# One block-fused kernel: the scan's first triangular inverse moved into the SSD stage, y times z at the evacuation, two barriers removed, the wout weights fetched later

## The chip, the cores and the metric

The kernel runs on one core of a Trainium2 chip. The metric is device time in microseconds (us). The core has TensorE (PE) for matmuls, VectorE (DVE), ScalarE (ACT), GpSimd (POOL) for elementwise work, and SyncE (SP), which only issues DMAs; ACT issues DMAs too. Each engine works its own instruction list in order and waits for others at semaphores.

## The reference

Two transformer-like blocks on 512 latent tokens. Only the first one's token mixers matter here. It projects the normalised input, runs a Mamba-2 style SSD scan and a gated DeltaNet (GDN) scan in two directions, gates and normalises both, and multiplies with `w_out`:

```
p = modulate(rmsnorm(x)) @ w_in          # z, xbc, dt, q k v, gate, a, beta
# SSD: chunks of 128 tokens, 16 heads
y = einsum(scores, xdt) + einsum(C, h_prev) * exp(acum);   ssd = xs * D + y (both directions)
v = ssd * silu(z);  v = v * rsqrt(mean(v * v over 512 channels)) * g
# GDN: T = I + strict(k_beta k^T * decay);  sol = triangular_solve(T, [v*b, k_beta*exp(g)])
v_new = u - w @ S;  o = q_dec @ S + qk @ v_new;  S = S * d + k_dec^T @ v_new
x = x + g1 * (concat(ssd_norm, gdn_norm(o) * silu(gate)) @ w_out)
```

Everything is float32. A large matmul takes its weights and its input as a high and a low part (`whi`, `wlo`), three passes for each product.

## The kernel before

**Stages.** The weights of all projections come as units of 128x1024 through two buffers: SP loads `raw`, ACT writes `whi` (L403 or L1786), DVE writes `wlo` (L410 or L2468), PE multiplies. The stages this text speaks of, with their place in the profiled execution, are these:

1. The zg stage, to 525 us: 16 units, first the 8 of z, then the 8 of the gate. PE runs one unit (24 matmuls) each round; ACT evacuates it (L1716) and stores it to `zg_scratch` (L1718). Beside it run the GDN pair masks (`AT`, stored to `at_scratch`), the SSD chunk states, and on DVE the inverses of the 32x32 diagonal blocks: `inverse_steps(n)` eliminates two columns (L2286, L2290) for the chains 0 and 1 (n below 16) or for chain 2 (n from 16). Their blocks (`UB`) come by small DMAs: most from SP (L741), 16 from ACT (`first_diagonals`, L1694).
2. `barrier(eng, 1)` (L355 to L358): PE, ACT, DVE and POOL drain, count up `phase_end` and wait until all four have. ACT first waits for its last stores to `zg_scratch`.
3. The SSD stage, 532 to 622 us: 4 chunks (`ci`) of 8 head pairs (`hp` on DVE and ACT, `b` on PE). For a pair PE makes the decays (L1100, L1101), ACT exponentiates them into `lbuf` (L1750, four), DVE makes `wmat` (L2383, L2384), PE makes y (L1117, L1120, L1125). PE makes the decays two pairs ahead. At a chunk's start stand the scores (L1085, ACT copies them to `stb`) and four selections (L1093) that DVE turns into `cpm` (L2373). ACT evacuates y into `yfm` (L1758), two halves for each chunk. `inverse_steps(16)` to `(31)` of chain 2 run on DVE from pair 2 of chunk 0 to pair 1 of chunk 2. SP then stores the inverses to `xb_scratch` and `xv_scratch` (L780 to L792).
4. `barrier(eng, 2)`.
5. The start of the GDN scan, 622 to 660 us. A scan step works on 4 groups `q`: 2 directions and 2 halves of the heads. A step's full inverse is put together from the 32x32 blocks by PE in four parts: `corner5` and `block5` (L1155), `corner6` and `block6_t` (L1179), with ACT copying corners to `PM` (L1774) and DVE copying blocks (L2409, L2412, L2419) between. Their operands are the mask `C` and the scattered blocks `DT`, `DB` (7 DMAs from SP for each q, L805 and L810, into buffers cleared before). For step 0 all this stands after the barrier and in front of the loop; so do z (loaded back whole, Silu, L1813), y times z (L2479), the squares (L1829), their sums (L1254), the roots (L1833 Ln, L1835 Exp), and the scaling with `ssdn` (L2484).
6. The scan, 660 to 789 us: steps 0 to 5, each `state_read` (L1220), `new_values` (L1138), `output` from step 2 on (L1239, L1240), `state_step` (L1138), `key_rows` (L1200), with the inverse parts of the next step between. At step 1 SP stores `yfm` to `y_scratch`; it comes back as `ynb` at the end.
7. The wout stage, from 789 us: units 0 to 5 take y (`yshi`, `yslo`), the others the GDN heads, which ACT and DVE normalise meanwhile (L1905, L1833, L1835, L1917, L2527, L2534). Units 0, 1 and 2 are loaded in the zg stage; unit 0 is split there and unit 1 after the second barrier.

**What sets the order.** All is written out by hand; there is no scheduler.

Of the kernel before, what the change touches and what calls it, by code (L numbers as in the profile page):

```python
# [18 lines left out]
P = 128  # L19
D = 1024  # L20
# [89 lines left out]
def layout(x, c, ctx, c_ctx, w_mod, b_mod, norm1_g, w_in, ssd_conv_w, ssd_conv_b, ssd_dt_bias, ssd_A_log,  # L110
# [22 lines left out]
    stream = {"qkvx": units(w_in, cols), "zg": units(w_in, np.concatenate([oz + r(1024), og + r(1024)]))}  # L133
# [101 lines left out]
def build_kernel(nc, a, out):  # L235
    ctx = ExitStack()
    with ctx:
# [106 lines left out]
        dve_done, act_done, phase_end = sem("dve_done"), sem("act_done"), sem("phase_end")  # L344
# [9 lines left out]

        def barrier(eng, n):  # L355

            eng.drain().then_inc(phase_end, 1)
            eng.wait_ge(phase_end, 4 * n)  # L358
# [72 lines left out]
        def room(n):  # L431
# [11 lines left out]
        grow = [at(f"grow{x}", kb, (P, 512), F32R) for x, kb in enumerate((203.125, 205.125, 164, 166, 168, 170, 76, 78))]  # L443
# [3 lines left out]
        S, DB0, DT1, DB1, C = ([at(f"{n}{q}", 36 + 8 * i + 2 * q, (P, 512)) for q in range(4)]  # L447
                              for i, n in enumerate(("S", "DB", "DT1", "DC", "C")))
        DB = (DB0, DB1)
        PM, DT0, KD, VN, QE, QKD, VB = ([at(f"{n}{q}", kb + 2 * q, (P, 512)) for q in range(4)] for n, kb in (  # L450
            ("PM", 140), ("DU", 148), ("KD", 156), ("VN", 164), ("QE", 172), ("QKD", 180), ("VB", 188)))
        DT = (DT0, DT1)
        ofm = at("ofm", 81, (P, GH * LAT))
# [18 lines left out]
        z_silu, gate_silu = ksum_full, tap_ready  # L472
        z_silu_0, gate_silu_0 = GH, 34
# [39 lines left out]

        def dcol(d, c, h=0):

            return (d * NCH + c) * NH + h
# [31 lines left out]
        zs = at("zs", 172, (P, KB * LAT))  # L548
        rsy = [at(f"rsy{g}", 203.125 + 2 * g, (P, LAT)) for g in range(2)]
        ynb = [at(f"ynb{s}", kb, (P, 4 * LAT)) for s, kb in enumerate((44, 156))]  # L550
# [116 lines left out]
        def _(sp_):  # L667
# [76 lines left out]
            for b in range(16):  # L744
# [5 lines left out]
                if b == 5:  # L750
                    sp_.wait_ge(v_stored, 16)
                if 5 <= b < 9:
                    load_diagonals(b - 5, 0)
                if b == 9:
                    load_diagonals(2, 1)
                    load_diagonals(3, 1)
# [15 lines left out]

            for job, j in tail[:3]:
                tail_load(job, j)
# [18 lines left out]

            store_inverse(0, (0,))
            store_inverse(1, (1,))
# [24 lines left out]
            def load_inverse(t, q):  # L820

                sp_.wait_ge(p5_full, 4 * (t - 1) + q + 1)
                if t == 1:
                    sp_.wait_ge(zeroed, 4 + q + 1)
                    sp_.wait_ge(db_zeroed, 4 + q + 1)
                else:
                    sp_.wait_ge(dr_full, 4 * (t - 2) + q + 1)
                    sp_.wait_ge(p6_full, 4 * (t - 2) + q + 1)
                load_dt(t, q)
                load_d32(t, q)  # L830

            sp_.wait_ge(zeroed, 4)
            sp_.wait_ge(xb_stored, 32)
            sp_.wait_ge(xv_stored, 32)
            for q in range(4):
                load_dt(0, q)
            store_mixed()
            sp_.wait_ge(phase_end, 8)
            sp_.wait_ge(db_zeroed, 4)
            for q in range(4):  # L840
                load_d32(0, q)
            for q in range(4):
                load_inverse(1, q)
# [13 lines left out]
            sp_.wait_ge(p6_full, 24)  # L857
            sp_.wait_ge(y_spilled, 16)
# [4 lines left out]
            sp_.dma_start(v3(gate, KB), zg_dram[KB:2 * KB].rearrange("b p n -> p b n")).then_inc(back_loaded, 16)  # L863
# [3 lines left out]
            for job, j in tail[3:]:  # L867
                tail_load(job, j)
# [11 lines left out]
        def _(pe):  # L880
# [198 lines left out]
            barrier(pe, 1)  # L1079

            for ci in range(4):
                c = NCTX + ci
                need(sc_copied, 1, lag=1)
                for gr in range(2):
                    mm = pe.matmul(bank[gr][:, 0:P], bf[64 * gr:64 * gr + 64, c * P:(c + 1) * P],  # L1085
                                   cfm[64 * gr:64 * gr + 64, ci * P:(ci + 1) * P], start=True, stop=True)
                mm.then_inc(sc_full, 1)
                if ci == 0:
                    pe.wait_ge(row_parts, 9)
                for m in range(4):  # L1090
                    need(cp_ready, 1, lag=2)
                    i = ci % 2 * 4 + m
                    pe.matmul(bank[2 + m % 2][:, :], halfsel[i // 4][:, i % 4 * P:(i % 4 + 1) * P], grow[4 + ci // 2][:, :], start=True, stop=True  # L1093
                              ).then_inc(cp_full, 1)

                def decays(hp):

                    need(l_ready, 1, lag=2)
                    bk = bank[4 + hp % 2]
                    pe.matmul(bk[:, :], cbf(0), b4(cbf(1, 2), 2), start=True, stop=False)  # L1100
                    pe.matmul(bk[:, :], rowcol(ci % 2 * 8 + hp), grow[2 + ci // 2][:, :], start=False, stop=True).then_inc(l_full, 1)  # L1101

                decays(0)
                decays(1)

                for b in range(KB):
                    if b + 2 < KB:
                        decays(b + 2)
# [1757 lines left out]
```

## Time and profile before

| | us |
|---|---|
| median of 3 runs | 2484.76 (2472.23 to 2487.89) |
| the profiled execution | 2470.89 |
| its span, first to last instruction | 2469.1 |
| PE busy | 2291.1 (93%) |
| DVE busy | 1354.3 (55%) |
| ACT busy | 984.4 (40%) |
| POOL busy | 150.7 (6%) |

In the rows further down a line of the timeline holds its start, its duration, the engine (SPq and ACTq are DMA issues), line of code, operation, output and input tiles, shape, count, and in brackets how long the engine stood idle before it and what released it. PEclk is the granted TensorE clock as a share of 2.4 GHz: 1.00 is 2.4 GHz and 0.50 is 1.2 GHz.

### The profile page before, as it was taken

The page shows a single profiled execution, that of the slowest core. Times are in us where ns is not written, and L with a number is a line of the kernel's source. Part 1 is how long each engine was busy: PE and PEld are TensorE (multiplying, and loading weights), DVE is VectorE, ACT ScalarE, POOL GpSimd, SP SyncE. Part 2 cuts the span into 40 slices and gives each one's busy share as a digit, 9 for nine tenths or more (in the row PEclk, how much of TensorE's full clock was granted, in tenths as well). Part 3 has the DMA queues.
Part 4 walks back from the last instruction along what each step waited for, and adds up shares of the span by engine and source line. Part 5 has one row for each costly group of instructions (what it writes and reads, how often), then busy time and mean ns, then how long its engine had stood idle before and what let it go on. Part 6 is the DMA issues. An engine that isn't in the chain of part 4 may idle for free.

```text
span 2469.1 us, 31028 instructions
## 1 busy us (share of the span) xinstructions
PE 2291.1 (93%) x12406; PEld 1831.3 (74%) x12406; DVE 1354.3 (55%) x2106; ACT 984.4 (40%) x1610; POOL 150.7 (6%) x108
## 2 busy tenths in 40 slices
PE   3899899989699889999998999999999899999997
PEld 2788787765588668888876568888888657888885
DVE  8566687677677345434455644444354564434445
ACT  3445455344524633322454544222234464322222
POOL 0000000000000010000032001000011302000002
PEclk9989999986899989999999999999999999999998
DMA  6233524630555223232232112232223202232232
GB/s 247 103 109 113 188 86 157 183 117 18 156 159 190 68 83 99 95 99 97 95 100 62 41 35 94 95 101 94 97 93 100 68 10 69 94 103 94 95 100 79
DMA packets 114495, 252.26 MB, mean 102 GB/s; under 512 B 45040, under 2 KB 45808, under 8 KB 113584
## 3 DMA queue, kind: packets, MB, share of 16 engines
q1 hardware_dynamic: 100896, 229.56, 28.1%
q10 hardware_dynamic: 13456, 20.71, 2.5%
q8 instruction: 99, 1.62, 0.3%
q14 instruction: 44, 0.36, 0.0%
HBM read 225.07 MB, written 25.17 MB: 101 GB/s over the span
## 4 chain that ended last, share of the span: by engine, by line
PE 78%; DVE 8%; ACT 6%; issue 3%; DMA 3%; SPq 1%; ACTq 1%; POOL 0%; DVEq 0%
PE bank L1306 18%; PE bank L1308 18%; PE bank L1307 18%; PE bank L966 4%; DVE cacc L2159 1%; DMA raw<-in_s_qkvx 1%; PE bank L1468 1%; PE bank L1457 1%; PE bank L1138 1%; PE bank L965 1%; DMA modw<-in_w_mod 1%; PE bank L1061 1%; PE bank L1063 1%; PE bank L1062 1%; PE bank L1125 1%
## 5 line engine op out<-in xcount | busy, mean ns | idle before, releaser
L1786 ACT ACTIVATE whi<-raw 128x1024 fp32r<-128x1024 f32 (+1 forms) x267 | 277.7, 1041 | 924.0 <-PE bank L1308 919.5
L1306 PE MATMUL bank<-ahi,whi 128*128 128x512 f32 x1152 | 454.6, 395 | 8.9 <-DVE alo L2588 6.0
L1307 PE MATMUL bank<-alo,whi 128*128 128x512 f32 x1152 | 450.6, 391 | 0.0
L1308 PE MATMUL bank<-ahi,wlo 128*128 128x512 f32 x1152 | 450.4, 391 | 0.0
L2468 DVE TENSOR_TENSOR wlo<-raw,whi 128x1024 fp32r<-128x1024 f32 (+1 forms) x267 | 327.3, 1226 | 132.8 <-ACT whi L1786 132.4
L1306 PE MATMUL bank<-bhi,whi 128*128 128x512 f32 x736 | 286.5, 389 | 0.0
L1308 PE MATMUL bank<-bhi,wlo 128*128 128x512 f32 x736 | 286.3, 389 | 0.0
L1307 PE MATMUL bank<-blo,whi 128*128 128x512 f32 x736 | 286.3, 389 | 0.0
L1306 PEld LDWEIGHTS bank<-ahi,whi 128*128 128x128 f32 x1152 | 217.7, 189 | 60.0 <-issue 11.3
L1307 PEld LDWEIGHTS bank<-alo,whi 128*128 128x128 f32 x1152 | 217.8, 189 | 46.1 <-issue 1.4
L1308 PEld LDWEIGHTS bank<-ahi,wlo 128*128 128x128 f32 x1152 | 217.7, 189 | 45.6
L2800 POOL TENSOR_TENSOR accx<-accx,sqr 128x512 f32<-128x512 f32 x42 | 72.3, 1722 | 1548.0 <-ACT sqr L1873 1342.7
L1306 PEld LDWEIGHTS bank<-bhi,whi 128*128 128x128 f32 x736 | 138.2, 188 | 28.9 <-issue 0.3
L1307 PEld LDWEIGHTS bank<-blo,whi 128*128 128x128 f32 x736 | 138.2, 188 | 28.7
L1308 PEld LDWEIGHTS bank<-bhi,wlo 128*128 128x128 f32 x736 | 138.2, 188 | 28.7
L2546 DVE TENSOR_TENSOR xr<-bank,xr 128x512 f32<-128x512 f32 x64 | 44.3, 692 | 159.5 <-PE bank L1308 159.5
L410 DVE TENSOR_TENSOR wlo<-raw,whi 128x1024 fp32r<-128x1024 f32 x51 | 62.3, 1222 | 95.5 <-ACT whi L403 95.2
L403 ACT ACTIVATE whi<-raw 128x1024 fp32r<-128x1024 f32 x51 | 54.1, 1063 | 150.6 <-DMA raw<-in_s_qkvx 76.6
L966 PE MATMUL bank<-hhi,whi 128*128 128x512 f32 x272 | 109.3, 402 | 0.0
L966 PE MATMUL bank<-hhi,wlo 128*128 128x512 f32 x272 | 108.4, 399 | 0.0
L966 PE MATMUL bank<-hlo,whi 128*128 128x512 f32 x272 | 108.1, 398 | 0.0
L2159 DVE SCALAR_TENSOR_TENSOR cacc<-cbuf,vec,cacc 128x784 f32<-128x784 f32 (+1 forms) x102 | 98.2, 963 | 10.7 <-ACT cacc L1611 7.9
(434 smaller groups left out, 3663.2 us busy)
## 6 DMA issues: line engine op xcount, KB each, us to landing
raw<-in_s_gu SPq DMA_DIRECT2D x88, 512.0 KB, 3.3
raw<-in_s_qkvx SPq DMA_DIRECT2D x34, 512.0 KB, 4.6
late_modw<-in_w_mod SPq DMA_DIRECT2D x32, 512.0 KB, 3.7
raw<-in_s_up SPq DMA_DIRECT2D x32, 512.0 KB, 3.3
raw<-in_s_down SPq DMA_DIRECT2D x32, 512.0 KB, 3.3
raw<-in_s_dn SPq DMA_DIRECT2D x32, 512.0 KB, 3.3
raw<-in_s_win SPq DMA_DIRECT2D x24, 512.0 KB, 3.3
raw<-in_s_zg SPq DMA_DIRECT2D x16, 512.0 KB, 3.5
```

Of the source, the lines that this page charges most:

```text
L403: act.activation(whi[k][:, 0:kc * P], raw[k][:, 0:kc * P], ACT.Identity).then_inc(hi_ready, 1)
L410: dve.tensor_tensor(wlo[k][:, 0:kc * P], raw[k][:, 0:kc * P], whi[k][:, 0:kc * P].bitcast(F32), ALU.subtract).then_inc(lo_ready, 1)
L965: pe.matmul(cx, w, x[:, s, 0:CTX], start=first, stop=last)
L966: mm = pe.matmul(lat, w, x[:, s, CTX:TOK], start=first, stop=last)
L1306: pe.matmul(out, w_hi, x_hi, start=start, stop=False)
L1307: pe.matmul(out, w_hi, x_lo, start=False, stop=False)
L1308: return pe.matmul(out, w_lo, x_hi, start=False, stop=stop)
L1786: act.activation(whi[u % 2][:, 0:width[u + 2] * P], raw[u % 2][:, 0:width[u + 2] * P], ACT.Identity).then_inc(hi_ready, 1)
L2159: after(dve.scalar_tensor_tensor(out=acc, in0=x, scalar=w, in1=acc, op0=ALU.mult, op1=ALU.add))
L2468: dve.tensor_tensor(wlo[u % 2][:, 0:width[u + 2] * P], raw[u % 2][:, 0:width[u + 2] * P], whi[u % 2][:, 0:width[u + 2] * P].bitcast(F32), ...
L2546: dve.tensor_tensor(blk(xr, b), bk[:, :], blk(xr, b), ALU.add).then_inc(taken, 1)
L2800: pool.tensor_tensor(acc[:, :], acc[:, :], sqr[n % 2][:, :], ALU.add).then_inc(sq_added, 1)
```

## The change

- The zg stage computes the gate's 8 units first and z's 8 last, and ACT evacuates z with Silu. It has no unit of wout behind it any more. ACT's 16 DMAs for `UB` go to SP; the inverse steps of chains 0 and 1 start one unit later and run two each round (0 and 1 at unit 8, 14 and 15 at unit 15).
- Both barriers are gone; single waits take their place.
- In the SSD stage DVE evacuates y times z in one instruction (`y_times_z`), with z loaded back by chunk (`load_z`); POOL squares it (`y_square`) and clears `DB` and `DT`.
- The four parts of step 0's inverse run on PE in chunk 2 (pairs 4 and 6) and chunk 3 (pairs 3 and 5), with their copies on ACT (pairs 5 and 4) and DVE (at the end of chunks 2 and 3). The blocks of steps 0 and 1, and the values of step 0, are fetched during the SSD stage.
- The scan starts with the square sums (four matmuls for each half), key rows for two of four groups and `corner5` of step 1. The roots' two Ln stand together, then the two Exp; POOL applies the roots (8 multiplies); the factor `ssdn` moves into the split of y after the scan.
- `C` and `DB` of the scan and `zc` lie at 0 to 24 KB, where `raw`, `whi` and `wlo` are, so the wout units 0 and 1 are loaded after the scan's last inverse and split after its last `new_values`; unit 2 is loaded behind the residual input `xr`.

```diff
-            eng.drain().then_inc(phase_end, 1)
-            eng.wait_ge(phase_end, 4 * n)
...
+        C, DB0, S, KD, PM, DT0, DT1, VN, QE, QKD, VB = ([at(f"{n}{q}", kb + 2 * q, (P, 512)) for q in range(4)] for n, kb in (
+            ("C", 0), ("DB", 8), ("S", 36), ("KD", 52), ("PM", 140), ("DU", 148), ("DT1", 156), ("VN", 164), ("QE", 172),
...
@@ SP
-            for job, j in tail[:3]:
-                tail_load(job, j)
...
+            load_z(0)
+            load_z(1)
...
+            sp_.wait_ge(y_taken, 2)
+            load_z(2)
+            sp_.wait_ge(y_taken, 4)
+            load_z(3)
             store_mixed()
...
             sp_.wait_ge(p6_full, 24)
+            for job, j in tail[:2]:
+                tail_load(job, j)
...
-            for job, j in tail[3:]:
+            for job, j in tail[2:]:
@@ PE
+                part = {(2, 4): corner5, (2, 6): block5, (3, 3): corner6, (3, 5): block6_t}.get((ci, b))
...
+                if ci == 3:
+                    pe.wait_ge(dt64_ready, 4)
...
+            def square_sums(gr):
+                pe.wait_ge(y_taken, 7 + gr)
+                pe.wait_ge(q_ready, 7 + gr)
...
+            square_sums(0)
+            key_rows(0, 0)
+            key_rows(0, 1)
+            corner5(1, 0)
+            corner5(1, 1)
+            square_sums(1)
@@ ACT
-                if b in (6, 7):
-                    first_diagonals(b - 6)
...
-            for k in range(2):
-                act.wait_ge(zg_stored[k], 8 * job.n)
-            barrier(act, 1)
...
+                if (ci, hp) == (2, 5):
+                    act.wait_ge(xb_stored, 64)
+                    act.wait_ge(xv_stored, 64)
+                    for q in range(4):
+                        corner(0, q, p5_full)
+                if (ci, hp) == (3, 4):
+                    for q in range(4):
+                        corner(0, q, p6_full)
+                        load_corners(1, q)
@@ DVE
-                if b >= 7:
-                    for n in range(max(0, 2 * b - 15), min(16, 2 * b - 13)):
+                if b >= 8:
+                    for n in range(2 * b - 16, 2 * b - 14):
                         inverse_steps(n)
...
+                dve.tensor_tensor(y_part(ci, gr), h4(bank[6 + gr][:, :]), h4(zc[ci % 2][:, 512 * gr:512 * gr + 512]), ALU.mult).then_inc(y_taken, 1)
...
+                    if hp == 5:
+                        y_times_z(ci, 0)
+                    if hp == 1 and ci:
+                        y_times_z(ci - 1, 1)
+                if ci >= 2:
+                    for q in range(4):
+                        (block5, block6_t)[ci - 2](0, q)
+            y_times_z(3, 1)
@@ POOL
+                pool.tensor_tensor(h4(xtm[:, o:o + 512]), y_part(ci, gr), y_part(ci, gr), ALU.mult).then_inc(q_ready, 1)
...
+                pool.tensor_tensor(blk(yfm, b), blk(yfm, b), rsy[b // 4][:, :], ALU.mult).then_inc(yn_ready, 1)
```

Three places show how the instructions move. The first is SP's queue where the zg stage goes over into the SSD stage. Before:

```order
L715 DMA raw_49<-in_s_zg 128x1024 [waits lo_ready,hi_ready]
L715 DMA raw_50<-in_s_zg 128x1024 [waits lo_ready,hi_ready]
L771 DMA raw_49<-in_s_wout 128x1024 [waits lo_ready]
L771 DMA raw_50<-in_s_wout 128x1024 [waits lo_ready]
L771 DMA raw_49<-in_s_wout 128x1024 [waits lo_ready]
L780 DMA xb_scratch<-XB_137 128x1024 [waits inv_done0]
L783 DMA xv_scratch<-XT_140 128x1024 [waits inv_done0]
```

Now:

```order
L713 DMA raw_50<-in_s_zg 128x1024 [waits lo_ready,hi_ready]
L833 DMA C_174<-at_scratch 128x512 [waits lo_ready,hi_ready]
L833 DMA C_175<-at_scratch 128x512
L833 DMA C_176<-at_scratch 128x512
L833 DMA C_177<-at_scratch 128x512
L779 DMA xb_scratch<-XB_137 128x1024 [waits inv_done0]
L782 DMA xv_scratch<-XT_140 128x1024 [waits inv_done0]
L779 DMA xb_scratch<-XB_138 128x1024 [waits inv_done1]
L782 DMA xv_scratch<-XT_141 128x1024 [waits inv_done1]
L827 DMA zc_222<-zg_scratch 128x8x128 [waits zg_stored1,zg_stored0,unit_done]
```

The three wout loads have left; the masks of step 0 and, behind the stores of the inverses, the first z of the SSD stage stand there.

The second place is ACT in chunk 2 of the SSD stage, pairs 5 to 7 (each pair is a row and a row of three more). Before:

```order
L1750 ACTIVATE lbuf_157<-bank,ng 128x128 [waits w_ready,l_full]
L1750 ACTIVATE lbuf_157<-bank,ng 128x128 x3
L1758 ACTIVATE yfm<-bank 128x4x128 [waits y_full]
L1750 ACTIVATE lbuf_156<-bank,ng 128x128 [waits w_ready,l_full]
L1750 ACTIVATE lbuf_156<-bank,ng 128x128 x3
```

Now:

```order
L1805 ACTIVATE lbuf_157<-bank,ng 128x128 [waits w_ready,l_full]
L1805 ACTIVATE lbuf_157<-bank,ng 128x128 x3
L1772 ACTIVATE PM_190<-bank 128x512 [waits p5_full,xv_stored,xb_stored]
L1772 ACTIVATE PM_191<-bank 128x512 [waits p5_full]
L1772 ACTIVATE PM_192<-bank 128x512 [waits p5_full]
L1772 ACTIVATE PM_193<-bank 128x512 [waits p5_full]
L1805 ACTIVATE lbuf_156<-bank,ng 128x128 [waits w_ready,l_full]
L1805 ACTIVATE lbuf_156<-bank,ng 128x128 x3
```

The copy of y is gone; four corner copies stand between the exponentials of pair 5 and pair 6, behind a wait for PE and for the stores of chain 2's inverses.

The third place is ACT at the end of the scan. Before:

```order
L1779 ACTIVATE VN_208<-bank 128x512 [waits dr_full]
L1779 ACTIVATE VN_209<-bank 128x512 [waits dr_full]
L1860 ACTIVATE yshi<-ynb_227 128x512 [waits yn_loaded0]
L1860 ACTIVATE yshi<-ynb_227 128x512 x3
L1860 ACTIVATE yshi<-ynb_228 128x512 [waits yn_loaded1]
```

Now:

```order
L1816 ACTIVATE VN_204<-bank 128x512 [waits dr_full]
L1816 ACTIVATE VN_205<-bank 128x512 [waits dr_full]
L1823 ACTIVATE whi_51<-raw_49 128x1024 [waits unit_done,raw_loaded0]
L1823 ACTIVATE whi_52<-raw_50 128x1024 [waits unit_done,raw_loaded1]
L1870 ACTIVATE yshi<-ynb_228,vec 128x512 [waits yn_loaded0]
```

Two splits of wout stand between the last new values and the high part of y.

## Rows read from the trace of the kernel before

**Rows 1.** Stretches: from:to, length, busy PE PEld DVE ACT POOL, clock, DMA, GB/s.
```profile
460.00:480.00 20.00, 16.46 (x68) 13.27 (x66) 6.74 (x19) 4.11 (x6) 0.00 (x0) 0.83 0.60 162
...
532.10:557.40 25.30, 22.30 (x154) 12.57 (x154) 20.92 (x52) 10.20 (x36) 1.91 (x4) 0.70 0.07 11
557.40:585.80 28.40, 27.69 (x156) 15.70 (x154) 21.55 (x54) 10.68 (x36) 0.00 (x0) 0.50 0.00 1
585.80:605.00 19.20, 18.49 (x156) 10.37 (x154) 12.40 (x29) 10.62 (x36) 0.00 (x0) 0.82 0.21 56
605.00:622.40 17.40, 15.97 (x154) 9.21 (x152) 9.97 (x21) 10.52 (x36) 0.00 (x0) 1.00 0.00 1
```
**Rows 2.** Timeline of ACT in the zg stage: the diagonal DMAs and the late split.
```profile
462.94 5.76 ACTq L1694 DMA_DIRECT2D UB<-at_scratch  x8
468.80 1.06 ACT L403 ACTIVATE whi<-raw 128x1024 fp32r<-128x1024 f32 x1 [6.33 <-issue]
```
**Rows 3.** Chain of waits at the first barrier: start, duration, what.
```profile
526.01 6.00 DMA zg_scratch<-stg
```
**Rows 4.** Timeline of DVE at the start of chunks 0 and 3 of the SSD stage.
```profile
538.01 0.43 DVE L2383 TENSOR_TENSOR wmat<-lbuf 128x256 f32<-128x256 f32 x1 [1.43 <-ACT lbuf L1750]
...
605.94 2.57 DVE L2373 TENSOR_TENSOR cpm<-bank,cfm 128x512 f32<-128x512 f32 x4 [1.70 <-PE bank L1093]
...
609.51 0.42 DVE L2383 TENSOR_TENSOR wmat<-lbuf 128x256 f32<-128x256 f32 x1 [1.00 <-issue]
```
**Rows 5.** Timeline of PE at 2.4 GHz: two SSD pairs, then the scan's start.
```profile
599.19 0.39 PE L1100 MATMUL bank<-cb 128*128 128x512 bf16 x1
...
600.92 0.39 PE L1100 MATMUL bank<-cb 128*128 128x512 bf16 x1
...
657.01 2.84 PE L1254 MATMUL bank<-zs,cf 128*128 128x512 f32 x6
659.69 1.95 PE L1138 MATMUL bank<-VB,DU 128*128 128x128 f32 x16
661.57 0.45 PE L1155 MATMUL bank<-PM,DT 32*32 32x32 f32 x32
...
670.69 0.68 PE L1179 MATMUL bank<-DC,C 64*64 64x64 f32 x16
...
674.57 2.05 PE L1220 MATMUL bank<-S,kf 128*128 128x128 f32 x16
```
**Rows 6.** Timeline of SP: the last store of chain 2's inverse.
```profile
596.48 1.10 SPq L792 DMA_DIRECT2D xv_scratch<-XT  x1
```
**Rows 7.** Its time from issue to landing, from the answer on its line.
```profile
DMA to landing us min/median/max: 3.9/3.9/3.9
```
**Rows 8.** Timeline of DVE and POOL: one operation alone, then beside one of POOL.
```profile
1232.87 0.75 DVE L2553 SCALAR_TENSOR_TENSOR alo<-xr,fm,ahi 128x512 fp32r<-128x512 f32 x1
...
1238.31 1.88 DVE L2553 SCALAR_TENSOR_TENSOR alo<-xr,fm,ahi 128x512 fp32r<-128x512 f32 x1
1238.34 1.29 POOL L2800 TENSOR_TENSOR accx<-accx,sqr 128x512 f32<-128x512 f32 x1 [2.14 <-ACT sqr L1873]
```
**Rows 9.** Timeline of the copies on ACT and DVE at the scan's start.
```profile
640.00 1.08 ACT L1774 ACTIVATE PM<-bank 128x512 f32<-128x512 f32 x2 [1.95 <-PE bank L1155]
640.33 0.28 DVE L2409 COPY DB<-bank 32x128 f32<-32x128 f32 x1 [8.95 <-PE bank L1155]
640.64 0.64 DVE L2412 STREAM_TRANSPOSE DU<-bank 32x128 f32<-32x128 f32 x2
...
648.47 4.90 DVE L2479 TENSOR_TENSOR yfm<-yfm,zs 128x512 f32<-128x512 f32 x8
```
**Rows 10.** Timeline of SP and ACT at the start of the wout stage.
```profile
790.56 51.18 SPq L771 DMA_DIRECT2D raw<-in_s_wout  x7
...
795.37 1.06 ACT L1786 ACTIVATE whi<-raw 128x1024 fp32r<-128x1024 f32 x1 [1.31 <-PE bank L1308]
```
**Rows 11.** Issue to landing of the first of those loads, issued at 790.56.
```profile
DMA to landing us min/median/max: 8.8/8.8/8.8
```

More of the change, by code:

```diff
@@ L1130, in _ @@
-            barrier(pe, 2)
-            A, B = bank[0:4], bank[4:8]
-            def four(dst, w, x):
-                for j in range(4):
-                    o = slice(j * P, (j + 1) * P)
-                    mm = pe.matmul(dst[:, o], w[:, o], x[:, o], start=True, stop=True)
-                return mm
-            def key(t, q, j):
-                h, c = 4 * (q // 2) + j, GSEQ[q % 2][t]
-                return kf[:, h * TOK + c * P:h * TOK + (c + 1) * P]
+            A, B = bank[0:4], bank[4:8]
@@ L1193, in block6_t, with first_inverse @@
                 quadrants(False, PM, DT[t % 2], e6t_full, p)
+            def first_inverse(ci, b):
+                if (ci, b) == (2, 4):
+                    pe.wait_ge(sc_copied, 3)
+                    pe.wait_ge(row_parts, 11)
+                part = {(2, 4): corner5, (2, 6): block5, (3, 3): corner6, (3, 5): block6_t}.get((ci, b))
+                if part is corner6:
+                    pe.wait_ge(sc_copied, 4)
+                if part is not None:
+                    for p in range(2):
+                        part(0, p)
@@ L1195, in key_rows, with four, key @@
+            def four(dst, w, x):
+                for j in range(4):
+                    o = slice(j * P, (j + 1) * P)
+                    mm = pe.matmul(dst[:, o], w[:, o], x[:, o], start=True, stop=True)
+                return mm
+            def key(t, q, j):
+                h, c = 4 * (q // 2) + j, GSEQ[q % 2][t]
+                return kf[:, h * TOK + c * P:h * TOK + (c + 1) * P]
             def key_rows(t, q):
@@ L1854, in _ @@
                         load_corners(t + 2, q)
+            split(JOB["wout"].u0 - 2)
+            split(JOB["wout"].u0 - 1)
             for b in range(KB):
@@ L2492, in _ @@
                     for q in range(4):
+                        if t == 0 and q == 2:
+                            key_rows(0, 2)
+                            key_rows(0, 3)
                         block5(t + 1, q)
+                else:
+                    split(JOB["wout"].u0 - 2)
+                    split(JOB["wout"].u0 - 1)
                 if lat:
```

415 lines of the change are left out of this document (203 added, 212 removed).

## The prediction, made before the changed kernel ran

> **What bounds the kernel now.** The page gives PE 93% of the span, so the change can only pay where PE waits or runs at half clock. I read the windows by stage first, then the chain of waits, then the timelines at the seams. The stretches of the SSD stage [rows 1] show the granted clock: 0.50 in chunk 1, 0.70 and 0.82 in chunks 0 and 2, 1.00 in chunk 3. Chunk 1 takes 28.4 us and chunk 3 17.4 us with the same pairs. Chunk 1's row holds two things: PE is busy 27.69 of 28.4, because its work takes twice as long at 1.2 GHz, and DVE has 21.55 us of work against 9.97 in chunk 3, because the inverse steps run beside it. The chain shows one clear stop, 6.00 us for a store to land in front of the first barrier [rows 3]. After chunk 3 ends at 622.4, PE does its first `new_values` at 659.69 and its first state read at 674.57 [rows 5]: 52.2 us in which it mostly waits for blocks from DRAM, for copies between the parts of one inverse, and for z, squares and roots.
>
> **Term A, the zg stage.** ACT issues 16 diagonal DMAs itself, the first 8 in 5.76 us, and the split of the next unit stands idle for 6.33 behind them [rows 2]. From 460 to 480 PE is busy 16.46 of 20 us at a mean clock of 0.83 [rows 1]: 3.54 us idle, and since 0.83 means 6.8 us at half clock, 3.3 of its busy time ran at half and cost another 1.6. So 5.1 us are lost. The DMAs now stand in SP's queue, ahead of the loads of the gate and z units, and DVE's inverse starts one unit later. SP issues 8 such DMAs in about 5 us where ACT took 5.76, which fits a round of 6 to 8 us, though closely. I take -5; bounds 0 (SP is late instead) and -6.
>
> **Term B, the first barrier.** Its 6.00 us store wait [rows 3] goes, as the first reader of z is five pairs into chunk 0. What is late next is the chain over DVE's `fq`, ACT, DVE, the first `xd` and `cpm`. In chunk 3 the first `wmat` follows the first `cpm` by 609.51 - 605.94 = 3.6 us at full clock [rows 4]. The last of PE's work before the barrier ends at 526.1; I give the eps chain and `xd` 2.4 us, so `cpm` starts at 528.5 and `wmat` at 532.1, where it was at 538.01 [rows 4]: -6. Bounds -4 and -7. ACT's change of table between Silu and Exp stands ahead of waits it has anyway, so I cost it at nothing; uncovered it would be one activation or two, within the bounds.
>
> **Term C, work put into the SSD stage.** One pair takes PE 600.92 - 599.19 = 1.73 us at full clock [rows 5].
> - Chunks 0 and 1, close to the limit on both engines: DVE gets three y times z of 4.90/8 = 0.61 to 0.7 us [rows 9] and POOL three squares. A collision of DVE with a POOL operation that reads two tiles cost DVE 1.88 - 0.75 = 1.1 us [rows 8]. 3 x (0.7 + 1.1) = 5.4; DVE's spare time at the chunk's start takes some: +3.3, bounds 0 and +5.4.
> - Chunk 2: PE gets `corner5` and `block5`, 4 x 0.45 = 1.8 [rows 5]. ACT copies four corners, 2 x 1.08 = 2.2 us [rows 9], ahead of pair 6's exponentials, where PE is only one pair ahead; less what PE does meanwhile that is +1.3. Before, the stores behind those copies were issued until 597.6 and landed 3.9 later [rows 6, 7], 601.5; now a z load of 0.5 MB and a y times z stand ahead of them, 2 us, while ACT wants them at about 601.7: +1.8. At the chunk's end DVE does four copies with two transposes each, 4 x 0.99 = 4.0 [rows 9], and PE waits for them; 1.70 of it was idle before [rows 4]: +2.3. Sum +7.2, bounds +4 and +12.
> - Chunk 3: `corner6` and `block6_t`, 4 x 0.65 = 2.6 from [rows 5], and +0.9 for four small copies and four DMAs in ACT's queue ahead of pair 5. +3.5, bounds +2.6 and +6. The last four DVE copies lie behind the first square sums.
>
> C is +14, bounds +7 and +23.
>
> **A rule on the ports.** The Trainium skill (SBUF — State Buffer, Who interferes with whom) says that a DVE instruction with two SBUF inputs and a GpSimd instruction that reads SBUF exclude each other, the later one waiting for the whole of the other; the trace agrees, with 1.88 us against 0.75 [rows 8]. By that rule `wmat` and the inverse steps can meet each of the squares while y times z, with one input in PSUM, cannot.
>
> **Term D, from the end of chunk 3 to the first state read, 52.2 us.** Now PE does four square-sum matmuls for half 0. Three took 2.84 [rows 5], so four take 3.8. Then key rows for two groups 1.0, `corner5` of step 1 0.9, the second square sums 3.8: `new_values` begins at +9.5. y times z (0.7) and POOL's square (1.3, [rows 8]) of the last half are done by +3, under the first sums. Then 1.95 and 0.45 [rows 5], key rows 1.0, a wait of 1.7 until DVE, which has two block copies first, has made the key rows of groups 2 and 3, `new_values` 2.0 and `block5` 0.45: +17. From there to the state read it is as before: two state steps, two `corner6`, key rows and two `block6_t`, 8.3 us. State read at +25.3 instead of +52.2: -26.9. Bounds -20 (if the blocks of step 1 or POOL are late) and -29. POOL's eight root multiplies end later than DVE's did, up to 13.6 us at 1.7, and SP holds step 3's blocks behind the store of y; the gap to step 3's `corner5` covers that by some 2 us.
>
> **Term E, the start of the wout stage.** ACT has two splits more (1.06 each, [rows 10]), DVE too, but its y parts keep ahead of PE's unit 0. Then ACT must split unit 2, which before was long there. SP now issues its load behind `xr`. Before, the load in that place was issued at 790.56 and landed 8.8 later, at 799.4 [rows 10, 11]; ACT's split began at 795.37. ACT's chain of Ln and Exp for the eight heads follows it in order and PE waits for the heads, so +4; bounds +2 and +5.
>
> **Sum.** -5 - 6 + 14 - 26.9 + 4 = -19.9 us. The profiled execution took 2470.9; this makes 2451. It lies 13.9 under the median of the runs shown, 2484.8, and I put the same difference there: 2465.
>
> **Rivals.**
> - *The clock stays at 2.4 GHz through the SSD stage.* For it: PE no longer stands 6 us before chunk 0. Against it: the clock fell in the middle of chunk 0, after having been full, when DVE prepared chain 2, and that is unchanged. DVE's 21.55 us in chunk 1 plus its waits at the chunk's start bound it at some 25; chunks 0 and 2 would win about 5 together: -8 more, 2457.
> - The Trainium skill (TensorE: Matmul & The Clock Gate, What's actually happening) says that sustained activity releases the clock and idleness drops it. By that rule chunk 1 should have recovered; PE was busy 27.69 of 28.4 us at 0.50 [rows 1], so here the trace does not follow it.
> - *The low clock lasts to the end of the stage and into the scan's start: slower.* Chunk 3 at half clock costs up to 28.4 - 17.4 = 11 us, the rest of chunk 2 some 8, and the 25 us of PE work behind it up to 12 more: +31 against -19.9, 2496. It decides from where it costs 20, that is if the clock does not recover in both chunks. For it: ACT's and DVE's new copies make PE stop every few pairs; against it, the recovery in chunk 2 before.
> - *A wait takes the gain:* the collisions, the late stores in chunk 2 and SP's queue each reach their upper bound (C at +23): 2474.
> - *The loads are hidden anyway:* E is 0 and the collisions miss: 2458.
>
> **How the numbers follow.** Forecast as summed 0.48; clock stays full 0.17; hidden loads 0.08; a wait takes the gain 0.17; low clock lasts 0.10. The range runs from 2446 to 2486. About 1% (24.8 us, below 2460) is what a measurement of this kernel can tell from no change. The full-clock case and the hidden loads lie mostly below it, the forecast in a quarter of its cases: 0.34 faster. Of the lasting low clock half is beyond +1%: 0.05 slower. The rest, 0.61, is the same.
>
> **What would show it.** A: no idle ACT ahead of the split near 468, z and gate rounds of 6.4 us. B: the first scores within 3 us of the last zg unit. C: chunk 2 some 7 us and chunk 3 some 3.5 us longer at equal clock, with ACT idle ahead of `PM` in chunk 2, PE waiting for a transpose at chunk 3's start, and `wmat` or elimination rows of over 1 us beside POOL's squares. D: `new_values` some 10 us after the last y, state read some 25. E: the third wout split some 4 us later against PE's unit 0, behind a DMA. The forecast fails if the granted clock of the SSD stage differs from [rows 1], or if the scan's steps 1 to 3 wait for `pre_loaded`.

## The result and the profile after

| us | before | after |
|---|---|---|
| median of 5 runs | 2484.76 (2472.23 to 2487.89) | 2458.13 (2457.58 to 2465.21) |
| the profiled execution | 2470.89 | 2457.67 |
| its span | 2469.1 | 2455.9 |

The five runs of before are the three that the prediction had and two more. The ratio is 0.9914, with a 95% interval of 0.9888 to 0.9940: by it the kernel is 21 us faster. The difference is 13.2 us between the two profiled executions and 26.6 between the medians. That these two differ by a factor of two is the main thing that the experiments had to explain.

The SSD stage of the changed kernel in windows, one for each chunk, then the stretch to the first state read (columns as in [rows 1]):

```profile
522.40:548.60 26.20, 21.50 (x155) 12.03 (x154) 22.97 (x56) 10.89 (x36) 4.36 (x8) 0.79 0.39 107
548.60:577.10 28.50, 25.36 (x155) 13.54 (x154) 24.11 (x56) 11.33 (x42) 4.15 (x6) 0.62 0.07 20
577.10:609.50 32.40, 30.02 (x283) 17.48 (x281) 17.68 (x44) 11.32 (x38) 4.05 (x6) 0.50 0.25 64
609.50:631.40 21.90, 20.26 (x217) 12.39 (x218) 14.23 (x28) 10.86 (x38) 2.30 (x2) 0.85 0.30 97
631.40:657.50 26.10, 24.25 (x304) 18.71 (x304) 12.56 (x28) 10.84 (x18) 8.14 (x7) 0.93 0.32 80
```

Against [rows 1] chunk 2 is 32.4 us instead of 19.2, and ran wholly at 1.2 GHz (0.50), where the trace of before shows 0.82. A stop is a stretch in which PE stands idle. The stops of over 1.5 us from the first `wmat` to the last y, from the timeline of PE:

```profile
536.57 0.44 PE L1215 MATMUL bank<-wmat,xtm 128*64 128x128 f32 x4 [2.23 <-DVE wmat L2425]
561.72 0.70 PE L1215 MATMUL bank<-wmat,xtm 128*64 128x128 f32 x4 [1.89 <-DVE wmat L2425]
609.50 0.80 PE L1177 MATMUL bank<-cfm,bf 64*128 64x128 f32 x4 [1.58 <-DVE DU L2374]
```

The first stood in the kernel before too, at 546.59 with 2.23 us. The granted clock went to 0.50 at 537.4, 0.8 us behind the first, and at 561.3, within the second. The scan's start, on PE, answers to [rows 5]:

```profile
631.29 3.70 PE L1306 MATMUL bank<-xtm,cf 128*128 128x512 f32 x8
640.04 1.95 PE L1232 MATMUL bank<-VB,DU 128*128 128x128 f32 x16
645.25 2.50 PE L1232 MATMUL bank<-VB,DU 128*128 128x128 f32 x16 [1.85 <-DVE KD L2444]
657.55 2.05 PE L1269 MATMUL bank<-S,kf 128*128 128x128 f32 x16
```

The wout stage begins at 772.53, and ACT's split of its third unit answers to [rows 10]:

```profile
782.46 1.06 ACT L1823 ACTIVATE whi<-raw 128x1024 fp32r<-128x1024 f32 x1 [2.78 <-DMA raw<-in_s_wout]
```

It stands 9.93 us behind PE's unit 0; before it was 795.37 - 789.54 = 5.83.

**The ledger.** Five marks in each trace divide the whole difference: the last square sums of the zg stage, the first `wmat`, the end of the last y, the first state read, and unit 0 of wout. The terms of the prediction against the first trace of before, and against a second one, told of below:

| us | predicted | against trace 1 | against trace 2 |
|---|---|---|---|
| A, to the end of the zg stage | -5 | -3.7 | -4.4 |
| B, to the first `wmat` | -6 | -6.4 | -6.5 |
| C, to the end of the last y | +14 | +18.9 | +6.5 |
| D, to the first state read | -26.9 | -25.9 | -25.9 |
| the scan to unit 0 of wout | 0 | 0.0 | 0.0 |
| E, from unit 0 to the end | +4 | +3.8 | +3.5 |
| sum | -19.9 | -13.2 | -26.7 |

### The profile page after: what moved, and what is told of

It is laid out like the page before. It is cut to its first block, busy times and chain, and to the rows that moved or that the text cites. A ratio compares the mean times of both kernels' runs of the same rounds, so it can differ in the third digit from the quotient of the medians.

```text
span 2455.9 us, 31012 instructions
## 1 busy us (share of the span) xinstructions
PE 2298.3 (94%) x12406; PEld 1834.7 (75%) x12406; DVE 1348.0 (55%) x2090; ACT 971.0 (40%) x1585; POOL 173.3 (7%) x132
## 4 chain that ended last, share of the span: by engine, by line
PE 79%; DVE 8%; ACT 5%; DMA 3%; issue 3%; SPq 1%; POOL 0%; ACTq 0%; DVEq 0%
PE bank L1351 19%; PE bank L1353 18%; PE bank L1352 18%; PE bank L989 4%; PE bank L1232 2%; DVE cacc L2170 2%; DMA raw<-in_s_qkvx 1%; PE bank L1513 1%; PE bank L1502 1%; PE bank L988 1%; DMA modw<-in_w_mod 1%; PE bank L1084 1%; PE bank L1086 1%; PE bank L1085 1%; PE bank L1220 1%
## 5 line engine op out<-in xcount | busy, mean ns | idle before, releaser
L1353 PEld LDWEIGHTS bank<-bhi,wlo 128*128 128x128 f32 x736 | 138.2, 188 | 28.8
L1351 PEld LDWEIGHTS bank<-bhi,whi 128*128 128x128 f32 x736 | 138.2, 188 | 28.8 <-issue 0.3
```

Source lines behind the costliest of these rows:

```text
L1351: pe.matmul(out, w_hi, x_hi, start=start, stop=False)
L1353: return pe.matmul(out, w_lo, x_hi, start=False, stop=stop)
```

## Experiments

Twelve kernels ran, two of them the kernels before and after once more, and each left one trace. The stretch from the first `wmat` to the end of the last y is called the stage's length: 84.4 us in the first trace of before, 103.4 in that of the changed kernel.

**The kernel before once more.**

> The kernel before, unchanged, for a second trace. Its profiled execution took 2470.9 us, its other runs 2472 to 2488. Theory A (the clock in chunk 2): a typical run of it stays at 1.2 GHz through chunk 2 of the SSD stage, where the first trace went back to 2.4 GHz at 592.5; a run of about 2485 us then shows a granted clock of about 0.5 there and chunk 2 about 28 us long instead of 19.2. Rival: the difference of 10 to 14 us lies in another stage (loads, ends of groups), and the SSD stage looks as in the first trace.

It took 2484.45 us. Its SSD stage in windows by chunk:

```profile
533.00:561.30 28.30, 27.59 (x152) 15.70 (x152) 21.06 (x52) 10.31 (x36) 1.89 (x4) 0.50 0.06 10
561.30:588.20 26.90, 24.48 (x154) 13.59 (x152) 21.45 (x54) 10.68 (x36) 0.00 (x0) 0.63 0.01 1
588.20:616.70 28.50, 27.78 (x156) 15.78 (x154) 12.49 (x29) 10.68 (x36) 0.00 (x0) 0.50 0.15 38
616.70:635.70 19.00, 18.25 (x154) 10.25 (x152) 9.97 (x21) 10.62 (x36) 0.00 (x0) 0.82 0.00 1
```

The stage is 96.8 us long, 12.4 more than in [rows 1], of the 13.5 by which the two spans differ; chunk 2 alone makes 9.3 of it. All other stretches agree within 1 us. So the kernel before has runs that differ by how long the clock stays at 1.2 GHz in this stage (43.9 us of the stage's length in trace 1, 77.5 in trace 2), and its 48 runs in this study, from 2468 to 2488 us, lie about half below and half above 2479. Their mean granted clock, on record for 43 of them, goes the same way: 0.963 to 0.970 in the runs under 2475 us and 0.956 to 0.964 in those over 2480; that they too lose it in this stage only the two traces show. The first trace was one of the good ones.

**Parts behind the stage.** All four parts of step 0's inverse, with their copies and corner loads, back behind the SSD stage (on PE, ACT and DVE alike):

```
-                    first_inverse(ci, b)
...
+            for spot in ((2, 4), (2, 6), (3, 3), (3, 5)):
+                first_inverse(*spot)
```

> The changed kernel with the four parts of step 0's inverse (corner5, block5, corner6, block6_t, with their copies and the corner loads of step 1) back behind the SSD stage; everything else stays, their blocks are loaded by then. Term D's theory, the parts cost more behind the stage than in it: chunk 2 and chunk 3 each lose their stops (1.58 us for a transpose, 0.9 to 2.2 for ACT's exponentials), together 5 to 8 us shorter at equal clock, and the first state read comes 12 to 16 us later than 26.2 us behind the last chunk (before, the parts took 636.19 to 649.84, 13.7 us, with all loads late): 5 to 9 us slower than the changed kernel. Rival, the stops in the stage drop the clock and cost as much as they save: within 2 us of the changed kernel.

2463.75 us (2460.72 to 2464.38), ratio to before 0.9913 (0.9896 to 0.9929). Chunks 2 and 3 in windows:

```profile
577.80:606.20 28.40, 27.69 (x155) 15.73 (x153) 14.54 (x32) 9.48 (x34) 4.06 (x6) 0.50 0.26 70
606.20:625.50 19.30, 18.59 (x158) 10.61 (x158) 12.45 (x23) 9.48 (x34) 2.19 (x2) 0.80 0.20 59
```

These are the lengths and clocks of the second trace of before, 28.5 and 19.0; the stage is 96.8 long, also the same. So the parts cost 6.6 us in the stage, and with the products and squares alone it is as long as before. Of it 68 us ran at 1.2 GHz, against 77.5 in the second trace of before, so what they cost in chunks 0 and 1 may be hidden in that difference. The parts do not cause the low clock in chunk 2, which is there without them. Behind the stage they cost 10.9 us (first state read at +37.1 instead of +26.2), a little less than expected. Their place is worth 4.3 us. The ratio does not resolve that; the marks of the traces do.

**The squares on ACT.** POOL's `y_square` goes, ACT does it behind the exponentials of pairs 3 and 7:

```
-                pool.tensor_tensor(h4(xtm[:, o:o + 512]), y_part(ci, gr), y_part(ci, gr), ALU.mult).then_inc(q_ready, 1)
...
+                act.activation(h4(xtm[:, o:o + 512]), y_part(ci, gr), ACT.Square).then_inc(q_ready, 1)
```

> The eight squares of y times z move from POOL to ACT, which has some 17 us free in every chunk. Theory B, POOL's squares hold back DVE: each of the wmat instructions that took 1.15 us beside a square takes 0.42 again, the stop of PE of 1.89 us at 559.8 in chunk 1 shrinks to about 1.1, and 0.7 to 3 us are won, 5 to 12 if the second fall of the clock, at 561, stays away with it. Rival, they cost nothing because PE at 1.2 GHz is the limit: within 1 us of the changed kernel, or up to 2 slower where a square stands ahead of an exponential in ACT's order.

2455.17 us (2452.61 to 2458.99), ratio 0.9920 (0.9894 to 0.9946). In the changed kernel the collision reads like this on DVE and POOL:

```profile
560.07 0.42 DVE L2424 TENSOR_TENSOR wmat<-lbuf 128x256 f32<-128x256 f32 x1
560.23 1.15 POOL L2808 TENSOR_TENSOR xtm<-yfm 128x512 f32<-128x512 f32 x1 [16.57 <-DVE yfm L2391]
560.52 1.14 DVE L2425 TENSOR_TENSOR wmat<-wmat,stb 128x256 f32<-128x256 f32 x1
```

Six of eight squares met a `wmat` so and held it for 0.73 us. With the squares on ACT none of them is left, and the stop of 1.89 us in chunk 1 is 1.16. In chunk 2 the clock came back (0.81), but the stage stayed at 103.0 us, for PE then ran into the next stop:

```profile
593.14 2.06 ACT L1772 ACTIVATE PM<-bank 128x512 f32<-128x512 f32 x4 [3.58 <-DMA xv_scratch<-XT]
595.07 2.20 ACT L1811 ACTIVATE lbuf<-bank,ng 128x128 f32<-128x128 f32 x8
```

```profile
597.21 0.44 PE L1215 MATMUL bank<-wmat,xtm 128*64 128x128 f32 x4 [3.14 <-DVE wmat L2437]
```

The first two rows are ACT: it waits 3.58 us for the store of chain 2's inverse, copies four corners, and only then makes the exponentials of pairs 6 and 7. The third is PE, which stops 3.14 us for them; the clock fell again. Time at 1.2 GHz in the stage's length went from 72 to 52 us and its length did not change. This trace is of the slowest of the five runs, 2458.99 us; the other four took 2452.61 to 2455.76. What the squares alone are worth in a typical run is therefore open.

**More PE work at the start of chunk 2.**

```
+                if ci == 2:
+                    pe.wait_ge(sc_copied, ci + 1)
+                    for _ in range(10):
+                        pe.matmul(bank[1][:, :], cbf(0), b4(cbf(1, 2), 2), start=True, stop=True)
```

> The changed kernel with ten matmuls of 128x512 bf16 more, whose result nobody reads, at the start of chunk 2 of the SSD stage, behind the first two decays. Chunk 2 ran wholly at 1.2 GHz in the changed kernel (33.3 us). Theory A, the clock comes back after a stretch in which PE streams wide matmuls without a stop: it is at 2.4 GHz from about 587 on, the pairs of chunk 2 take 1.73 to 2 us instead of 3.05, the ten matmuls cost 4, net 5 to 9 us faster. Rival, the clock comes back at a time that has nothing to do with this work: 2 to 4 us slower, chunk 2 still at 0.50.

2455.8 us (2454.37 to 2462.76), ratio 0.9926 (0.9898 to 0.9954). The clock did come back in chunk 2 (0.74), and the chunk took 28.8 us in spite of the extra work. But it also came back there, at 0.73, in two kernels without this work (the next one, and the one with the diagonals on ACT). A stop of 1.78 us for ACT's corner copies followed, the clock fell, and chunk 3 took 25.7 us. In this trace nothing was won. It is of a run of 2461.59 us, and three of the other four took 2454.37 to 2455.80, so neither a gain nor whether the extra matmuls brought the clock back is settled.

**The third wout unit's load ahead of xr.**

```
+            tail_load(*tail[2])
             sp_.wait_ge(r_ready, 20)
             sp_.wait_ge(o_full, 16)
...
-            for job, j in tail[2:]:
+            for job, j in tail[3:]:
```

> The load of the third wout unit stands ahead of the load of xr in SP's queue. Theory C, the 4 us that the wout stage lost at its start are the wait of ACT for this load: ACT's split of that unit, 9.9 us behind PE's unit 0 in the changed kernel, comes at about 6, and the kernel is 3 to 4 us faster. Rival, ACT's order of roots, not the load, sets the pace: the split comes earlier but the heads do not, within 1 us.

2457.44 us (2452.71 to 2460.32), ratio 0.9921 (0.9897 to 0.9945). ACT's split comes without a wait, 7.06 us behind unit 0:

```profile
783.70 1.04 ACT L1824 ACTIVATE whi<-raw 128x1024 fp32r<-128x1024 f32 x1
```

From unit 0 to the end it is 1680.2 us instead of 1683.4; before it was 1679.6. So the load was term E, nearly whole. The gain of 3.2 us is too small for the ratio to show.

**The start of chain 2 spread over chunk 0.** The fill behind `cpm`, one copy behind pair 0, one behind pair 1:

```
+                if ci == 0:
+                    chain2_start(0)
...
+                    if ci == 0 and hp < 2:
+                        chain2_start(hp + 1)
```

> The start of chain 2's inverse on DVE (a fill, two copies, 2.8 us in one piece behind pair 2 of chunk 0) is spread: the fill behind the cpm products of chunk 0, one copy behind pair 0 and one behind pair 1. Where the clock was full there, PE stood 2.23 us in the middle of chunk 0, in the kernel before and in the changed one, and the clock fell 1 to 2 us later. Theory A: no stop over 1.3 us in chunk 0, the clock stays at 2.4 GHz into chunk 1, chunk 0 takes 19 to 22 us instead of 26, 3 to 6 us faster. Rival, DVE limits chunk 0 at either clock, since a pair with its steps takes it some 2.7 us: the stops only spread, chunk 0 takes 24 to 26 us, within 2 us.

2458.63 us (2455.73 to 2462.23), ratio 0.9897 (0.9882 to 0.9912). Chunk 0 ran at a clock of 0.95 and took 24.7 us, of which PE was busy for 18.6 only: DVE has 22.8 us of work in it. The clock fell at the end of it, as PE stopped 2.13 us behind a square. The stage took 103.4 us. The rival is right for chunk 0: DVE's sum of work is the limit at the full clock, and the full clock gains little there. Chunk 1 ran at 0.62 here; in the last run below it takes 27.0 us at 0.82 with 22.7 of DVE work, which points the same way.

**The store wait back.**

```
+            for s in range(2):
+                pe.wait_ge(zg_stored[s], 16 * 8)
```

> The changed kernel in which PE waits for the stores of z and the gate ahead of chunk 0 again, nothing else of the barrier. Term B says that this wait alone cost the 6.35 us: the first wmat comes 12 to 13 us behind the last square sums of the zg stage instead of 6.5, and the clock is at 0.50 there for some us. Rival, the rest of the barrier (four engines drained, ACT's wait) took part of it: 9 to 11 us.

One run, 2461.58 us. The chain of waits answers to [rows 3]:

```profile
519.44 3.92 DMA zg_scratch<-stg
```

The first `wmat` is 10.7 us behind the last square sums, against 12.8 before and 6.5 in the changed kernel. The 10.7 lie in the rival's range of 9 to 11, but the rest of the barrier is not the reason: from the end of the wait to `wmat` it is 5.9 us as before, and the 2.1 that are missing are the store itself, 3.92 us instead of 6.00. So the wait costs 4.2 with this store, and a slower store made the rest. Before, SP's wout loads ran beside it; that this slowed it was not tried.

**The first diagonals on ACT.** `first_diagonals` back in ACT's list, `load_diagonals(1, 1)` and `(0, 1)` out of SP's:

```
+                if b in (6, 7):
+                    first_diagonals(b - 6)
```

> The changed kernel with the first sixteen diagonal loads back in ACT's queue, in two lots of eight ahead of a split. Term A says that they alone cost the zg stage its 3.7 us: the last square sums come at about 525 instead of 521.5, with PE idle near 470. Rival, the one unit less between DVE's inverse steps and the stage's end, or the order of gate and z, made the difference: 521 to 522.

One run, 2459.75 us. The last square sums come at 523.3, between the 521 to 522 of the rival and the 525 of the theory. From the traces, the rounds of the last nine zg units (the time between ACT's evacuations) are 7.9, 9.9, 7.4 and six of 6.4 before; 5.5, 5.9, 7.1, 7.3 and five of 6.4 in the changed kernel; 6.2, 8.9 and seven of 6.4 here. Near 470 the diagonals in ACT's queue cost 3.7 us more than none there (6.2 and 8.9 against 5.5 and 5.9); over all nine rounds they cost 2.1, for in SP's queue they make a stop of their own. So their place explains 2.1 of the 5.8 us by which the nine rounds became shorter. The other 3.7 are gone with the diagonals on ACT too. In this run ACT issued the first eight in 4.05 us instead of 5.76 and PE stopped 1.84 us for them instead of 3.54, the clock was at 1.2 GHz for 3.4 us instead of 6.8, and a second stop of 0.91 us at 481.3, for a `wlo` behind DVE's inverse steps, is missing. How much of this the later start of those steps made, and how much differs from run to run, was not tried. This is the stop that the burst in SP's queue makes, on SP, ACT and PE of the changed kernel:

```profile
469.11 8.68 SPq L739 DMA_DIRECT2D UB<-at_scratch  x16
477.89 0.36 SPq L713 DMA_DIRECT2D raw<-in_s_zg  x1
```

```profile
481.54 1.06 ACT L398 ACTIVATE whi<-raw 128x1024 fp32r<-128x1024 f32 x1 [3.50 <-DMA raw<-in_s_zg]
```

```profile
484.00 0.47 PE L1084 MATMUL bank<-hhi,whi 128*128 128x512 f32 x1 [1.48 <-DVE wlo L405]
```

Sixteen diagonals take SP 8.68 us, more than a round; the next unit's load is late behind them. In nine other traces with this order PE stopped there for 1.5 to 3.0 us, in one it did not.

**The changed kernel again, and two mended versions of it,** on one chip. `order_mended` has four moves in the queues: the wout load (SP), the corner copies (ACT), the corner loads (from ACT to SP) and the stores of chain 2 (SP):

```
+            tail_load(*tail[2])
...
-            for job, j in tail[2:]:
+            for job, j in tail[3:]:
...
-                if (ci, hp) == (2, 5):
+                if (ci, hp) == (2, 6):
...
-                if (ci, hp) == (3, 4):
+                if (ci, hp) == (3, 5):
...
-                        load_corners(1, q)
...
+            for q in range(4):
+                sp_.wait_ge(p6_full, q + 1)
+                sp_.wait_ge(pre_loaded[q], 240)
+                sp_.dma_start(C[q][:, :], at_dram[pair_of(q, 1)]).then_inc(pre_loaded[q], 16)
...
+            store_mixed()
             sp_.wait_ge(y_taken, 4)
             load_z(3)
-            store_mixed()
```

`order_and_dve` has these, the squares on ACT and the spread start.

> The changed kernel as it is, beside the two that follow on the same chip. Its SSD stage took 103.4 us with 72 us of it at 1.2 GHz in its first trace, and 103 to 106 in five others that differ from it in one point each, with 51 to 75 us at 1.2 GHz. If the stage's length no longer depends on the clock, since PE waits for DVE and ACT where the clock is full, this trace shows 102 to 106 us again, and the times lie within 8 us of one another, where those of the kernel before lay 16 to 18 apart. Rival: some run of it gets the clock back in chunk 2, as the kernel before did, and is 10 us faster.

> The changed kernel with four moves in the order of the queues: the third wout unit's load ahead of xr on SP; ACT's copies of the corners one pair later in chunks 2 and 3; the corner loads of step 1 from ACT's queue to SP's; the stores of chain 2 ahead of the last z load. Expected: the wout stage starts 3 us earlier; the stop of PE for ACT's exponentials in chunk 3 (0.93 to 2.7 us) goes, the transposes at the end of chunk 2 (1.6) stay. 3 to 6 us faster than the changed kernel. Rival: the clock decides and these stops are hidden at 1.2 GHz: 2 to 3 us, that of the wout load alone.

> The same, with the two edits that take load off DVE's worst places: the squares of y times z on ACT, and the start of chain 2's inverse spread over chunk 0. If the stops of PE behind DVE in chunks 0 to 2 keep the clock down and the clock matters, 5 to 15 us faster than the changed kernel, with less than 50 us at 1.2 GHz in the SSD stage. If DVE's sum of work is what holds chunks 0 to 2 at full clock (some 2.7 us a pair with an inverse step against 3.05 of PE at 1.2 GHz), no more than 1 or 2 us beyond the kernel with the order alone.

| | median us | ratio to before | stage's length | of it at 1.2 GHz |
|---|---|---|---|---|
| changed_again | 2462.56 | 0.9934 (0.9911 to 0.9958) | 104.8 | 71 |
| order_mended | 2455.95 | 0.9917 (0.9892 to 0.9942) | 104.7 | 84 |
| order_and_dve | 2448.20 | 0.9879 (0.9856 to 0.9903) | 95.4 | 53 |

The changed kernel repeats itself: 103.4 and 104.8 for the stage, seven runs within 7.6 us where 12 of before lie 17 apart. One of the seven, 2455.74, lies 5.2 us below the next; no trace shows why. The new order alone takes the stops behind ACT away (no stop over 0.5 us between 566.1 and 613.5, nor in chunk 3), but at 1.2 GHz they cost nothing, and the stage is as long as before; its gain is the wout load (7.06 us again) and lies inside the intervals.

**Which of the two DVE edits it is.** `order_and_squares` is `order_and_dve` without the spread start.

> The four moves in the queues and the squares on ACT, but the start of chain 2 in one piece as in the changed kernel. If it was POOL's squares (each holds a wmat instruction back by 0.7 us) that kept PE stopping, and with it the clock down in chunk 2, the SSD stage takes 94 to 98 us with chunk 2 at 24 to 26, and the kernel needs 2446 to 2451. If it was the spread start, chunk 2 is at 30 to 32 us and at 0.50 again, and the kernel needs 2454 to 2458.

2451.62 us (2446.88 to 2455.07), ratio 0.9883 (0.9860 to 0.9906); the profiled execution took 2449.46. Its SSD stage by chunk:

```profile
523.70:553.20 29.50, 27.56 (x157) 15.62 (x156) 22.42 (x56) 11.38 (x37) 3.19 (x7) 0.54 0.34 94
553.20:580.20 27.00, 20.97 (x155) 10.72 (x154) 22.68 (x56) 12.56 (x44) 1.91 (x4) 0.82 0.07 21
580.20:604.60 24.40, 20.12 (x283) 11.69 (x282) 16.78 (x43) 12.56 (x40) 1.91 (x4) 0.85 0.33 77
604.60:625.30 20.70, 19.99 (x217) 12.36 (x217) 13.26 (x28) 11.87 (x40) 0.00 (x0) 0.84 0.39 113
```

The stage is 95.4 us long, as with the spread start, which thus adds nothing in these two traces; the ratios, 0.9879 and 0.9883, do not tell the two versions apart either. Chunk 2 is 24.4 instead of 32.1 to 32.4. In the nine other traces with the parts in the stage its length is 103.0 to 106.8. They read as if the two edits need each other: with the squares on ACT alone the clock came back in chunk 2 and was lost to the stop behind ACT's copies (103.0); with the order alone it did not come back (104.7); with both it came back and stayed until the transposes at the chunk's end (95.4).

The times show a part of this. On one chip the six runs of `order_and_dve` (2442.56 to 2449.69) all lie below the six of `order_mended` (2451.50 to 2463.22). They do not show that either edit alone is worth nothing: on that chip, though not in the same round, the squares alone had a median 7.4 us under `changed_again`, the order alone 6.6, and `order_and_dve` 14.4, which is close to plain addition. That each needs the other rests on one trace of each alone. These two versions are the best measured here, each with its median 30 us under that of the kernel before on its chip. Beyond the changed kernel they win 8 to 9 us in the SSD stage and 3 in the wout stage.

## Why the prediction was right, and where it was not

The time of 2458.13 us lies 7 under the 2465 that were predicted, and in the range. "The same", within 1%, was the likeliest outcome with 0.61, and the ratio of 0.9914 is in it; the median itself lies under the 2460 where the prediction drew its line. The sum of -19.9 us stands between the -13.2 and the -26.7 of the two traces of before.

That the number came so near is in part luck. The prediction says that it fails if the granted clock of the SSD stage differs from [rows 1]. It did: 0.79, 0.62, 0.50 and 0.85 in the four chunks, for 0.70, 0.50, 0.82 and 1.00. Two errors then stood against each other: the change of the trace was put 6.7 us too good, and the step from the trace to the median 13.4 us too large.

- **The base.** The prediction took 2451 for the trace's own time and put the same 13.9 us on top for the median. The trace of the changed kernel gave 2457.7, 6.7 above; the median 2458.1, 6.9 below. The step that failed is that constant: the 13.9 us were not something that every kernel carries, but mostly the clock in the SSD stage (12.4 of the 13.5 us between two traces of before), which this change touches. The spread of the three runs shown, 2472 to 2488, was the sign that something in the kernel has two lengths.
- **A, right in sum, in part for another reason.** The idle time ahead of the split near 468 is gone. The bound "SP is late instead" came true in part: the prediction put 8 diagonals into a round, about 5 us, but SP had 16 in one, 8.68 us, and two of the rounds are 7.1 and 7.3 us, not 6.4. The last nine rounds are 5.8 us shorter than before, and the stage's earlier part ended 2.1 us later, upstream of the change, which leaves -3.7. Of the 5.8 only 2.1 are shown to be the place of the diagonals.
- **B, right.** The first scores stood at 522.41, 0.9 us behind the last square sums; -6.4 against -6. Of it 4.2 are the wait, 2.1 the slow landing of that one store.
- **C, mis-sized against the first trace, +18.9 for +14.** Against a trace with the same clock in chunk 2 it is +6.5, nearly all of it from the parts: chunk 2 grows by 3.9, of which `corner5` and `block5` take PE 2.0 (1.8 put down, at full clock) and the wait for the transposes 1.58 (2.3); chunk 3 grows by 2.9, of which the two other parts take 2.2 and a stop for exponentials 0.93. Chunks 0 and 1, put at +3.3 together, come out at -0.3. The collisions are there, 0.73 us each and not 1.1, but PE at half clock hides most of them. The late stores, put at +1.8, cost nothing here: SP had issued the last of them at 590.26, and what ACT waited for was PE's own `corner5`:

```profile
599.00 2.06 ACT L1772 ACTIVATE PM<-bank 128x512 f32<-128x512 f32 x4 [4.70 <-PE bank L1114]
```

Its copies, put at +1.3, did not stop PE in this chunk. Where the clock was back in chunk 2, with the squares on ACT, ACT waited 3.58 us for the store and PE stopped 3.14 behind the copies. What the term lacked was that these costs and the clock are one question: at 1.2 GHz a pair takes PE 3.05 us and covers DVE and ACT; at 2.4 GHz it takes 1.73 and PE stops behind them.
- **The rival "low clock lasts"** was given 0.10 and came true by half: chunk 2 stayed low to its end, chunk 3 recovered after some 6 us, and of the 26 us to the first state read some 3.5 were low. It was priced against a kernel that recovers in chunk 2. The second trace of before does not, and by its times about half of its runs do not, so against these it was no loss.
- **The ports.** The rule of the Trainium skill (SBUF — State Buffer, Who interferes with whom) held in the trace: a `wmat` whose inputs both lie in SBUF waited for POOL's square, 1.15 us for 0.42, six times, and ended 0.3 us behind it; the products of y and z, with one input in PSUM, took 0.68 to 0.69.
- **D, right.** `new_values` at +8.7 (predicted +9.5), the wait for the key rows of groups 2 and 3 1.85 us (1.7), the state read at +26.2 (+25.3). In seven of the other traces, with the clock full throughout, it is +24.7. Step 3's blocks behind the store of y were at the edge, as said: no wait in this trace, 1.19 us in the next one of the same kernel.
- **E, right.** +4.1 in the split's place, +3.8 to the end, and the load was the cause.

Left open: why the clock comes back at one chunk's start and not at another. In all traces of the changed order it came back near the start of chunk 1; in chunk 2 it did in some and not in others, though up to there they differ in little. The Trainium skill (TensorE: Matmul & The Clock Gate, What's actually happening) has sustained activity release the clock and idleness drop it. The falls in the stage agree so far: they followed stops of 1.2 to 3.1 us. But not every stop brought one: the clock stayed at 2.4 GHz behind stops of 2.21, 2.09 and 2.23 us in chunk 3 of `changed_again`, of the kernel with the squares on ACT and of the one with the wout load first. The rises do not agree by themselves: PE was busy 30.0 of 32.4 us in chunk 2 at 0.50.

## What to carry to other kernels

Where repeated runs of a kernel spread by more than its measurement should, find the stage in which they differ before pricing a change: a difference between the profiled run and the median is not a constant. In a stage where PE runs at half clock, waits of the other engines can be hidden: here ACT's corner copies made no stop of PE where chunk 2 ran at 1.2 GHz, and one of 3.14 us where the clock was back. So one trace in which an edit changes nothing does not show that it is worth nothing, and edits that act on the same stage should be tried together as well; two such took 8 to 9 us off the stage in the traces here. A late load or a moved burst of small DMAs is priced by its queue: 16 of them took SP 8.7 us, and the next large load waited behind them.

## What was not expected of the hardware

- Stops of PE of 2.23 and 1.89 us were followed by more than 15 and 50 us at 1.2 GHz, with PE busy nearly all the time in the second case.
- The store of a 128x512 tile landed in 3.92 us in one kernel and in 6.00 in another, with other loads beside it.
- A POOL square with both inputs the same tile took 1.04 to 1.15 us, less than the two-tile sums of [rows 8], and held a DVE instruction by 0.73.
